# The MLP of a decoder step in two phases through memory, its down projection by Strassen's seven products

## What is computed

```python
h2 = rms_norm(x, g_ffn) * (1.0 + sc2) + sh2
x = x + ga2 * (jnp.square(jax.nn.relu(h2 @ w_up)) @ w_down)   # w_up 1024 x 4096, w_down 4096 x 1024
y = rms_norm(x, g_final)
```

## Time and profile before

| | |
|---|---|
| time, median of 3 runs | 1790.4 us (1789.59 to 1791.74) |
| span of the profiled execution | 1786.6 us |
| its own time | not listed beside its span; the runs' median lies 3.8 us above the span (3.0 to 5.1) |
| matmul busy | 1653.8 us (93%), 10864 matmuls |
| weight loads busy | 1445.7 us (81%), beside the matmuls |
| VectorE, ScalarE, GpSimd busy | 726.3, 594.2, 428.4 us |
| mean granted TensorE clock | 0.954 of full |
| moved by DMA | 166.6 MB, 93 GB/s over the span |

### The profile page before, as it was taken

One profiled execution on the slowest core, in us unless ns is written; L12 is line 12 of the kernel. 1 busy time (PEld: TensorE's weight loads), 2 busy tenths in 40 slices (PEclk: granted clock), 3 DMA queues, 4 the chain that ended last, 5 costly groups with the idle time before them and its releaser, 6 DMA issues. The chain is left out here.

```text
span 1786.6 us, 27593 instructions
## 1 busy us (share of the span) xinstructions
PE 1653.8 (93%) x10864; PEld 1445.7 (81%) x10864; DVE 726.3 (41%) x1158; ACT 594.2 (33%) x1010; POOL 428.4 (24%) x304
## 2 busy tenths in 40 slices
PE   5999997999979999588699899999999999999997
PEld 2898996777755555266599799999999999999997
DVE  3511021444457777477314733232323232323225
ACT  3511121333248788244335421203021212121123
POOL 0122112222300000200255532423142323333230
PEclk8899998999989999677799999999999999999999
DMA  9123126667420000854633211111111111111102
GB/s 336 49 100 106 52 101 203 220 193 220 138 107 25 24 1 1 260 191 149 197 108 105 72 48 48 29 42 47 47 47 47 47 47 39 38 41 47 48 12 101
DMA packets 116400, 166.62 MB, mean 93 GB/s; under 512 B 6970, under 2 KB 80141, under 8 KB 116054
## 3 DMA queue, kind: packets, MB, share of 16 engines
q1 hardware_dynamic: 111088, 148.58, 25.5%
q0 software_dynamic: 5120, 16.78, 3.0%
q10 hardware_dynamic: 102, 0.03, 0.0%
HBM read 143.03 MB, written 22.35 MB: 93 GB/s over the span
## 5 line engine op out<-in xcount | busy, mean ns | idle before, releaser
L469 PE MATMUL psum<-op_hi,out_hi 128*128 128x384 f32 (+1 forms) x960 | 320.8, 334 | 10.0 <-DVE out_lo L137 8.1
L471 PE MATMUL psum<-op_hi,out_lo 128*128 128x384 f32 (+1 forms) x960 | 314.4, 328 | 0.0
L470 PE MATMUL psum<-op_lo,out_hi 128*128 128x384 f32 (+1 forms) x960 | 314.4, 327 | 0.0
L469 PE MATMUL psum<-mlp_a_hi,out_hi 128*128 128x384 f32 (+1 forms) x768 | 251.0, 327 | 0.5 <-DVE x1T L2648 0.5
L471 PE MATMUL psum<-mlp_a_hi,out_lo 128*128 128x384 f32 (+1 forms) x768 | 250.8, 327 | 0.0
L470 PE MATMUL psum<-mlp_a_lo,out_hi 128*128 128x384 f32 (+1 forms) x768 | 250.5, 326 | 0.0
L2538 POOL TENSOR_TENSOR out_lo<-out_raw,out_hi 128x2048 fp32r<-128x2048 f32 x31 | 143.2, 4621 | 271.7 <-ACT out_hi L2561 271.7
L2634 DVE TENSOR_TENSOR mlp_sq<-mlp_relu 128x384 f32<-128x384 f32 (+1 forms) x96 | 88.4, 921 | 279.8 <-ACT mlp_relu L2576 279.8
L469 PEld LDWEIGHTS psum<-op_hi,out_hi 128*128 128x128 f32 x960 | 181.6, 189 | 14.2 <-DVE out_lo L137 8.5
L470 PEld LDWEIGHTS psum<-op_lo,out_hi 128*128 128x128 f32 x960 | 181.5, 189 | 2.5
L471 PEld LDWEIGHTS psum<-op_hi,out_lo 128*128 128x128 f32 x960 | 181.4, 189 | 0.0
(11 more groups left out here) (342 smaller groups left out, 2977.5 us busy)
## 6 DMA issues: line engine op xcount, KB each, us to landing
sa_k<-in_cache_k SPq DMA_DIRECT2D x64, 256.0 KB, 3.1
sa_v<-in_cache_v POOLq DMA_DIRECT2D x64, 256.0 KB, 3.9
out_raw<-in_w_up SPq DMA_DIRECT2D x16, 1024.0 KB, 5.3
out_raw<-in_w_down SPq DMA_DIRECT2D x16, 1024.0 KB, 4.9
out_raw<-in_w_ada SPq DMA_DIRECT2D x26, 512.0 KB, 4.7
out_raw<-in_w_out SPq DMA_DIRECT2D x12, 1024.0 KB, 4.8
in_raw<-in_w_in SPq DMA_DIRECT2D x8, 1024.0 KB, 5.9
ada_w<-in_w_ada SPq DMA_DIRECT2D x3, 2048.0 KB, 13.6
```

The lines of the kernel that those rows point to most:

```text
L469: pe.matmul(out, w_hi, x_hi, start=(k == 0), stop=False)
L470: pe.matmul(out, w_hi, x_lo, start=False, stop=False)
L471: return pe.matmul(out, w_lo, x_hi, start=False, stop=(k == nk - 1))
```

## The change

The MLP becomes two phases.

**Up.** All 16 panel pairs of `w_up` (256 hidden features, two row tiles each), six groups each, in straight code, over eight banks. The squares go unrounded to `aq`, 128 x 2 x 1088, two buffers. For the first 15 pairs the two row tiles and the two token halves of 544 are the four blocks of a matrix; GpSimd forms the five sums or differences of them that Strassen's products need (`token_sums`), and SP stores these five and the two single blocks to memory (`aT`, 7 x 15 x 128 x 544, 29 MB). Pair 15 is stored whole (`a_last`).

**Down.** The 15 pairs are taken in chunks of 4, 4, 4 and 3, and each chunk by seven products: 28 items. `w_down`'s blocks are row tile parity by output half; a quadrant of 4 row tiles by 512 outputs is 1 MB, two sets of four. Per item:

- SP loads the token tile of up to four pairs (1.1 MB, three buffers), after the item three before it is done (`load_t`); ScalarE rounds it (`t_hi`), GpSimd makes the remainder (`t_lo`).
- For five of the seven products VectorE adds or subtracts two quadrants (`weight_sum`), after the item two before it is done; then ScalarE rounds (`weight_hi`), and GpSimd makes the remainder, or VectorE for the two products with one quadrant (`weight_lo`).
- TensorE: eight banks of 272 tokens by 128 outputs, three matmuls per pair, so 96 (in the last chunk 72). Products p7 and p6 go on accumulating in the banks of p1 and p3.
- VectorE adds each bank with its sign to one or two places of `x1T`; sample columns go to `csamp` and are gated in the direct part (`evacuate`).

**Direct part.** The last two row tiles over all of `LASTD` as before, two k tiles per group, with the final norm between. Its additions also fold in `csamp`.

New buffers lie over old ones (`over`): token tiles over `h_hi`, `aq` and the sums, quadrants over `w.raw`, `h_lo` and `aq`. A row of `PRODUCTS` has the name, the weight quadrants (output half, parity, sign), the token blocks (parity, token half, sign), whether it goes on in the same banks, and the outputs (output half, token half, sign). Core of the diff:

```diff
+PRODUCTS = [
+    ("p4", [(1, 1, 1)], [(1, 0, 1), (0, 0, -1)], False, [(0, 0, 1), (1, 0, 1)]),
+    ("p1", [(0, 0, 1), (1, 1, 1)], [(0, 0, 1), (1, 1, 1)], False, [(1, 1, 1)]),
+    ("p7", [(0, 1, 1), (1, 1, -1)], [(1, 0, 1), (1, 1, 1)], True, [(0, 0, 1)]),
+    ("p2", [(1, 0, 1), (1, 1, 1)], [(0, 0, 1)], False, [(1, 0, 1), (1, 1, -1)]),
+    ("p3", [(0, 0, 1)], [(0, 1, 1), (1, 1, -1)], False, [(0, 1, 1)]),
+    ("p6", [(1, 0, 1), (0, 0, -1)], [(0, 0, 1), (0, 1, 1)], True, [(1, 1, 1)]),
+    ("p5", [(0, 0, 1), (0, 1, 1)], [(1, 1, 1)], False, [(0, 0, -1), (0, 1, 1)]),
+]
...
+    CHUNK = [4, 4, 4, 3]
+    items = [(n, i) for n in range(len(CHUNK)) for i in range(NPROD)]
...
             def _(sp):
...
+                    if p == NPAIR - 1:
+                        sp.wait_ge(w.lo_done, NPAIR)
+                        load_quad(0, (0, 0))
+                        sp.wait_ge(s_tst, 16 * NSUM * (NPAIR - 1))
+                        sp.wait_ge(s_aq[0], 16 * NPAIR)
+                        sp.wait_ge(s_aq[1], 16 * (NPAIR - 2))
+                        load_t(0)
+                        load_t(1)
+                    sp.wait_ge(s_sq, UPG * (p + 1))
+                    if p < NPAIR - 1:
+                        sp.dma_start(aT[SINGLE[0], p], aq[p % 2][:, 0, 0:NH]).then_inc(s_aq[p % 2], 16)
+                        sp.dma_start(aT[SINGLE[1], p], aq[p % 2][:, 1, NH:T]).then_inc(s_aq[p % 2], 16)
+                        sp.wait_ge(s_tm, NSUM * (p + 1))
+                        for x, q in enumerate(SUMMED):
+                            sp.dma_start(aT[q, p], ts[:, x]).then_inc(s_tst, 16)
...
+                        sp.dma_start(a_last, aq[p % 2][:]).then_inc(s_al, 16)
+                sp.wait_ge(s_mm, NUP)
+                load_quad(0, (0, 1))
+                load_t(2)
+                load_quad(0, (1, 0))
+                for at in ((1, 1), (0, 0)):
+                    load_quad(1, at)
+                sp.wait_ge(s_al, 16)
+                for at in ((0, 1), (1, 0)):
+                    load_quad(1, at)
+                for i in range(3, NI + 1):
+                    sp.wait_ge(s_mm, mm_done(i - 3))
+                    load_t(i)
+                    n = i // NPROD + 1
+                    if i % NPROD == 2 and 2 <= n < len(CHUNK):
...
+                            load_quad(n, at)
...
             def _(pool):
+                for p in range(NPAIR - 1):
+                    pool.wait_ge(w.hi_done, p + 2)
+                    pool.tensor_tensor(w.lo[(p + 1) % 2][:], w.raw[(p + 1) % 2][:], w.hi[(p + 1) % 2][:], ALU.subtract).then_inc(w.lo_done, 1)
+                    token_sums(p)
+                t_lo(0)
+                t_lo(1)
+                t_lo(2)
+                for i in range(1, NI):
+                    weight_lo(i + 1)
+                    if i + 2 <= NI:
+                        t_lo(i + 2)
...
             def _(act):
+                for p in range(NPAIR):
...
+                    else:
+                        weight_hi(0)
+                        t_hi(0)
+                    for i, m, c in up_groups(p):
...
+                        act.activation(r[i % 3][:, 0:tw], g.bank[i % 8][:, 0:tw], ACT.Relu).then_inc(s_re, 1)
+                t_hi(1)
+                weight_hi(1)
+                t_hi(2)
+                for i in range(1, NI):
+                    weight_hi(i + 1)
+                    if i + 2 <= NI:
+                        t_hi(i + 2)
...
             def _(dve):
+                weight_sum(1)
+                weight_lo(1)
...
+                for i in range(NI):
+                    for k in range(ITG):
+                        evacuate(i, k)
+                        if k == 1 and i > 0:
+                            weight_lo(i + 1)
+                    weight_sum(i + 2)
...
             def _(pe):
-                pe.sem_inc(s_mm, NGR)
...
+                for i in range(NI):
+                    at_least(pe, s_sld, lows(i, True))
+                    at_least(pe, s_slp, lows(i, False))
+                    pe.wait_ge(s_tlo, i + 1)
...
+                            pe.wait_ge(s_ad, ops_through(i - 1, k))
+                        cols, toks = slice(m * P, (m + 1) * P), slice(s * NQ, (s + 1) * NQ)
+                        for j in range(pairs(i)):
+                            last = products(g.bank[k][:, 0:NQ], hi[:, j, cols], lo[:, j, cols], th[:, j, toks], tl[:, j, toks],
+                                            j == 0 and not goes_on, j == pairs(i) - 1)
+                        last.then_inc(s_mm, 1)
```

More of the change, by code:

```diff
@@ new lines, in stage_mlp_and_final @@
+        nga = g.sb("mlp_minus_gate", [P, KD], ctx=ctx)
+        flat_ts = ts[:].rearrange("p a t -> p (a t)")
+        early = [flat_ts[:, i * 384:(i + 1) * 384] for i in range(6)]
+        n2.buffers(early[0:4], early[4:6])
+        last_chunk = range(2 * KD, 3 * KD)
+        aT = nc.dram_tensor("mlp_aT", [NPROD, NPAIR, P, NH], F32, kind="Internal").ap()
+        a_last = nc.dram_tensor("mlp_a_last", [P, 2, T], F32, kind="Internal").ap()
+        four = lambda t: t.rearrange("p (j t) -> p j t", j=4)
@@ L2431, in stage_mlp_and_final @@
+        S_HI = [t[:].rearrange("p k c -> p (k c)") for t in w.hi]
+        S_LO = [t[:].rearrange("p k c -> p (k c)") for t in w.lo]
+        S_RAW = [g.over(f"mlp_s_raw{i}", W4, F32, w.lo[i]) for i in range(2)]
         s_mm = g.sem("mlp_group_summed")
@@ L2504, in _, with load_quad @@
[L2504 to L2512 removed]
+                def load_quad(n, at):
+                    half, par = at
+                    j0 = sum(CHUNK[:n])
+                    rows = w_down.rearrange("(j two p) c -> two p j c", two=2, p=P)[par]
+                    sp.dma_start(QUADS[n % 2][at][:, 0:CHUNK[n]], rows[:, j0:j0 + CHUNK[n], half * 512:(half + 1) * 512]).then_inc(s_q[n % 2][at], 16)
@@ L2550, in _ @@
                         n2.low_pool(pool, j)
-                blocks(pool, split, work)
+                for p in range(NPAIR - 1):
[9 more added lines that the diff above has]
+                        t_lo(i + 2)
@@ L2582, in _, with t_hi @@
+                def t_hi(i):
+                    if i in (1, 2):
+                        act.wait_ge(s_mm, NUP)
+                    if i > 2:
+                        act.wait_ge(s_mm, mm_done(i - 3))
+                    wait_t(act, i)
+                    act.copy(T_HI[i % 3][:, 0:rows_of(i)], four(T_RAW[i % 3])[:, 0:rows_of(i)]).then_inc(s_thi, 1)
                 for j in last_chunk:
                     n2.high(act, j)
-                blocks(act, split, work)
+                for p in range(NPAIR):
+                    if p + 1 < NPAIR:
+                        act.wait_ge(w.loaded[(p + 1) % 2], 16 * ((p + 1) // 2 + 1))
+                        at_least(act, s_mm, UPG * p)
+                        act.copy(w.hi[(p + 1) % 2][:], w.raw[(p + 1) % 2][:]).then_inc(w.hi_done, 1)
+                    else:
+                        weight_hi(0)
+                        t_hi(0)
+                    for i, m, c in up_groups(p):
+                        tw = CHUNKS[c][1]
+                        act.wait_ge(s_mm, i + 1)
+                        at_least(act, s_sq, i - 2)
+                        act.activation(r[i % 3][:, 0:tw], g.bank[i % 8][:, 0:tw], ACT.Relu).then_inc(s_re, 1)
@@ new lines, in _ @@
+                for p in range(NPAIR):
+                    pe.wait_ge(w.lo_done, p + 1)
+                    for i, m, c in up_groups(p):
+                        t0, tw = CHUNKS[c]
+                        at_least(pe, s_re, i - 7)
+                        if p == 0 and c == 2 and m == 0:
+                            n2.wait_chunk(pe, 2)
+                        cols = slice(m * P, (m + 1) * P)
+                        for k in range(KD):
+                            last = three_products(pe, g.bank[i % 8][:, 0:tw], w.hi[p % 2][:, k, cols], w.lo[p % 2][:, k, cols],
+                                                  h_hi[:, k, t0:t0 + tw], h_lo[:, k, t0:t0 + tw], k, KD)
+                        last.then_inc(s_mm, 1)
```

407 lines of the change are left out of this document (239 added, 168 removed).

## The result

The changed kernel takes 1770.4 us (1769.99 to 1770.93, four runs) against 1790.0 us (1786.37 to 1791.74) before: ratio 0.9892, 95% interval 0.9878 to 0.9906. That is 1.1% faster. The forecast was 1775.2 us, with a range of 1756 to 1794.

What follows compares the result with a forecast made beforehand. The MLP was taken as bound by TensorE's stream of matmuls. Terms of -40.4, -1.9, +7.6, +13.5, +2 and +4 sum to -15.2 us: span 1786.6 to 1771.4, plus 3.8 for the median, 1775.2 us, range 1756 to 1794.

Steps and rivals of the forecast that it cites:

- forecast A: Whole kernel: the turn and the summed weights cost some 20 us, giving 1775 us (1766 to 1786); chance 0.50.
- matmuls: Down phase and direct part: 2520 matmuls of 272 columns at 124.6 ns plus two direct row tiles, -40.4 us.
- start: First up matmul: its wait for VectorE's opening semaphore increment goes, -1.9 us (0 if another opening wait replaces it).
- up phase: Up projection: splits, sums, stores and loads stay hidden beside the matmuls, 0 us.
- turn: From up to down: late token tiles, splits and weight sums stall the first items, +13.5 us.
- steady waits: Down items: successive summed weights form a chain of 13.9 us per 12.0 us item; with small extras, +7.6 us.
- clock: Behind the turn's two long stalls: matmuls may run at reduced granted clock, +2 us (0 to 5).
- tail: Last third of the direct part: VectorE has more work per pair of groups than TensorE, +4 us (2 to 8).
- rival E: Down phase: narrow matmuls pay no fixed 6.6 ns each, 16.6 us lower, 1759 us; chance 0.06.
- Rival B: Down phase: loads and chain are hidden, only the first stalls and a short tail remain, 1757 us; chance 0.17.
- Rival C: Down phase: evacuations fall behind and the chain sets every item, 1818 us; chance 0.16 for over 1794.
- D: Down phase: the turn costs double, or half of Rival C holds, 1787 to 1794 us; chance 0.11.

Runs made afterwards that it cites:

- after: The changed kernel itself, as against the kernel before the change: 1770.4 us.
- short_split: Changed kernel, but from item 3 on GpSimd makes the token remainder of only one row tile, which TensorE reads for all: 1766.6 us.
- halves: Changed kernel with GpSimd's token split made by two instructions in place of one, from the fourth item on: 1764.7 us.
- p2_dve: Changed kernel with the weight remainder of product p2 made by VectorE in place of GpSimd: 1768.2 us.
- direct: Changed kernel with eight direct products, without sums, in place of Strassen's seven, in the same two phases: 1795.4 us.
- turn_loads: Changed kernel with one quadrant and token tile 2 loaded ahead of the store of the last squares: 1766.0 us.
- relu_first: Changed kernel with five relus of pair 15 ahead of ScalarE's copy of token tile 0: 1766.6 us.
- tile0: Changed kernel with token tile 0 loaded ahead of the second quadrant and its remainder made by VectorE in place of GpSimd: 1768.4 us.

## Why the prediction was right

The forecast A came in: 1770.4 for 1775.2. By its own steps:

| term | forecast | measured in the trace | 
|---|---|---|
| matmuls | -40.4 | -38.2 |
| start | -1.9 | -0.5 |
| up phase | 0 | 0 |
| turn | +13.5 | +9.8 |
| steady waits | +7.6 | +4.8 |
| clock | +2 | +3.1 |
| tail | +4 | +2.3 |
| stages ahead of the MLP | 0 | +2.5 |
| sum | -15.2 | -16.2 (span: -17.4) |

The sum leaves 1.2 us of the span's 17.4 without a row. The row of the matmuls prices the kernel before by the one stretch of the earlier trace rows; over its whole MLP, slow ones left out, matmuls of 384 and 320 columns stand 174.0 and 146.3 ns apart, some 3 us more in all, and those of the kernel after 173.6 and 146.5, 1.2 us more.

- **Matmuls.** The line through the earlier trace rows gave 124.6 ns, and four items without a wait took 124.7. Over all items it is 125.5, 2.2 us in all: behind each of the seven waits some 0.1 us is lost at the first matmul, the rest is spread over the items. The fixed part per matmul is real, and rival E falls. The Trainium skill's N/2.4 + 2.5 ns ("TensorE: Matmul & The Clock Gate", section "Back-to-back issue gap"), which the page gives as the gap of an isolated matmul, would have been 115.8; the trace disagrees by 9 ns.
- **Start.** The wait didn't go, it changed hands: 1.37 us behind TensorE's own sequencer for 1.86 behind VectorE's. "0 if another opening wait takes its place" was nearer.
- **Up phase.** No wait in 2304 matmuls, beside 75 sums and 105 stores. Right.
- **Steady waits.** The mechanism is the one of the prediction, period 13.7 for 13.9, and short_split and halves take all five waits away, p2_dve the three before items 10, 17 and 24. The mis-sized term is the loss per run: 1.4 us in a run of three for 2.1, since 0.2 us less in a period and 0.05 more in an item count twice; 1.8 in the last chunk for 2.7; 0.2 at the direct part for 0.5; nothing for the 0.2 of the quadrants.
- **Turn.** Before item 0 I had 2.1 and it was 5.2. I charged 2.7 us from the sums' end to the loads' issue, a single store's landing; five stores in a row, 2.4 us to issue, made it 5.1. And tile 0's load took 7.0 us with a quadrant's issued 2.7 us ahead of it, not 5.3. That delay then covered what I had charged behind it: nothing for 1.2 before item 1, 4.7 for 5.9 before item 2. Before item 3 nothing for 4.3: four quadrants were issued by 1411.4, and the DMA moved 409 GB/s from 1410 to 1420, not the 308 of the earlier trace rows, so tile 3 came at 1425.0 (35.4 us after the up phase, not 38), and item 2, itself late, ended 4.2 us later than I had it.
- **Clock.** The matmuls behind the two long waits stood 0.23 us apart for some 3.4 us each; items 0 and 2 took 13.58 and 13.64 us, where 96 matmuls at 125.5 ns are 12.05, so 1.5 to 1.6 us were lost per wait, where I had 2 for both. The granted clock was 0.83 in both stretches of 10 us, which mixes full speed with about half, 1.2 of 2.4 GHz. Kernel after, table of stretches, which answers to the earlier trace rows:

```profile
1390.00:1400.00 10.00, 5.12 (x29) 5.15 (x30) 9.15 (x7) 4.63 (x8) 6.13 (x2) 0.83 0.19 72
1420.00:1430.00 10.00, 5.33 (x31) 5.13 (x30) 7.88 (x10) 5.19 (x4) 7.46 (x2) 0.83 0.63 246
```

- **Tail.** +2.3 for +4. I charged VectorE's whole excess over TensorE in four pairs; the trace has two waits, 2.1 and 0.9 us, where before had 1.0, 1.0 and 0.5. In direct, with eight products, it is as long.
- **Ahead of the MLP** the stages took 2.5 us more in this trace, where nothing was changed; I have no cause, only the spread of 1004.6 to 1011.8 over the traces. It happened to be offset in the time: the median lies 1.2 us above the span, not 3.8. In each run here that has both, the time lies 1.6 to 2.0 us above the span of the same execution. So of the 3.8 us that I added some 2 were no part of the kernel: the profiled execution of before was that much shorter than the median one.

Rival B (1757) falls as well: of the four stalls of the turn two were hidden, but not the other two, and turn_loads, relu_first and tile0 shorten these by moving single links. Rival C (1818) falls: in after no item waits for additions to `x1T`. So does D. The forecast was 5 us too high by errors that partly cancel, which was luck: turn, steady waits and tail, 25.1 together, measured 16.9, in the turn because a delay ahead was added to one behind that it hides; matmuls, start, clock and the stages ahead took 7.2 of these 8.2 back; the offset between median and span gave 2.6, and 1.2 has no row.
